# One planned PSUM placement and five reorderings of engine work in a two-block transformer kernel on one core

## The reference, cut to what matters

```
mod = c @ w_ada + b_ada                          # six rows: shift, scale, gate, twice
h = rms_norm(x, g) * (1 + sc1) + sh1
proj = h @ w_in                                  # q, k, v for compressed, selected, window and indexed attention
o_nsa = gates * (attention to compressed keys, to selected blocks, to a window)
score = sum_h w_idx[h] * relu(q_idx[h] @ k_idx.T)     # index scores, top 64 keys of a token kept
o_dsa = attention to the kept keys
x = x + gt1 * rms_norm(concat(o_nsa, o_dsa) @ w_out)
x = x + gt2 * rms_norm(square(relu(h2 @ w_up)) @ w_down)
# second block
proj = rms_norm(x) @ w_in_2                      # stick breaking attention, gated recurrence, memory attention
mixed = concat(rms_norm(sb_o), rms_norm(hg_o) * silu(g), mem_o)
x = x + mixed @ w_out_2
x = x + peer_ffn(rms_norm(x))                    # 8 heads pick 16 of 16384 experts each
```

## Time and profile before

| | us |
|---|---|
| median of 3 runs | 1515.25 |
| lowest, highest | 1513.32, 1517.54 |
| the profiled execution | 1512.21 |
| its span in the trace | 1510.4 |

### The profile page before, as it was taken

The page is one execution under the profiler, slowest core; times in us unless marked ns, Lnnn a source line. Parts: engine busy times, 40 slices in busy tenths (PEclk is TensorE's granted clock), DMA queues, the critical chain, the costliest instruction groups (busy, mean ns, idle before and its releaser), DMA issues.

```text
span 1510.4 us, 23097 instructions
## 1 busy us (share of the span) xinstructions
PE 1419.9 (94%) x9108; PEld 1230.4 (81%) x9108; DVE 873.0 (58%) x1501; ACT 745.1 (49%) x1368; POOL 981.9 (65%) x710
## 2 busy tenths in 40 slices
PE   5798998999998899899999999999999999999998
PEld 2676777799786897679998999899997888888886
DVE  5655773555524786621889939999894343322222
ACT  2442223666445657444554464455554555555554
POOL 0567624566764553145899998778886777766675
PEclk9896899999999999999999999999999999999999
DMA  9442223455654332034544555555656666555552
GB/s 382 150 167 112 112 112 140 167 172 190 253 197 165 140 118 106 28 112 170 206 171 156 175 186 184 179 181 179 203 182 218 234 248 244 208 185 182 192 195 84
DMA packets 48588, 263.78 MB, mean 175 GB/s; under 512 B 5472, under 2 KB 14048, under 8 KB 19040
## 3 DMA queue, kind: packets, MB, share of 16 engines
q1 hardware_dynamic: 38272, 251.68, 46.3%
q10 hardware_dynamic: 10208, 10.63, 2.0%
HBM read 252.84 MB, written 9.44 MB: 174 GB/s over the span
## 4 chain that ended last, share of the span: by engine, by line
PE 65%; DVE 16%; POOL 3%; issue 1%; ACT 1%; PEld 0%; PEldq 0%; DVEq 0%; ACTq 0%
PE bank L1381 24%; PE bank L788 22%; PE bank L752 16%; DVE arena L2613 4%; DVE hotg L2613 4%; DVE arena L2609 3%; POOL v_lo L1912 3%; DVE hots L2609 2%; PE bank L1161 1%; DVE arena L2625 1%; DVE arena L2495 1%; PE bank L769 0%; DVE hT_lo L1969 0%; PEld bank L788 0%; PE bank L1327 0%
## 5 line engine op out<-in xcount | busy, mean ns | idle before, releaser
L1912 POOL TENSOR_TENSOR v_lo<-ring,v_hi 128x512 fp32r<-128x512 f32 x448 | 620.3, 1402 | 168.9 <-ACT v_hi L1812 160.4
L1904 POOL TENSOR_TENSOR v_lo<-ring,d_hi 128x512 fp32r<-128x512 f32 x213 | 294.7, 1395 | 303.5 <-ACT d_hi L1503 238.1
L1812 ACT CAST v_hi<-ring 128x512 fp32r<-128x512 f32 x512 | 315.4, 621 | 307.7 <-PE bank L1381 164.3
L752 PE MATMUL bank<-hT_hi,v_hi 128*128 128x256 f32 x1024 | 294.8, 288 | 5.4 <-POOL v_lo L1912 5.3
L752 PE MATMUL bank<-hT_lo,v_hi 128*128 128x256 f32 x1024 | 286.3, 280 | 0.0
L752 PE MATMUL bank<-hT_hi,v_lo 128*128 128x256 f32 x1024 | 286.1, 279 | 0.0
L1503 ACT CAST d_hi<-ring 128x512 fp32r<-128x512 f32 x236 | 144.0, 621 | 172.3 <-PE bank L788 148.9
L1381 PE MATMUL bank<-v_hi,mix_hi 128*128 128x512 f32 x512 | 202.5, 396 | 3.2 <-DVE mix_lo L2640 3.2
L1381 PE MATMUL bank<-v_hi,mix_lo 128*128 128x512 f32 x512 | 201.9, 394 | 0.0
L1381 PE MATMUL bank<-v_lo,mix_hi 128*128 128x512 f32 x512 | 201.9, 394 | 0.0
L752 PEld LDWEIGHTS bank<-hT_hi,v_hi 128*128 128x128 f32 x1024 | 192.4, 188 | 7.1 <-POOL v_lo L1912 4.2
(11 more groups left out here) (329 smaller groups left out, 2437.5 us busy)
## 6 DMA issues: line engine op xcount, KB each, us to landing
ring<-w_dram SPq DMA_DIRECT2D x230, 1024.0 KB, 4.8
gate_dram<-gput ACTq DMA_DIRECT2D x64, 128.0 KB, 3.1
gget<-gate_dram SPq DMA_DIRECT2D x32, 256.0 KB, 5.0
x<-x_dram SPq DMA_DIRECT2D x1, 1024.0 KB, 5.5
arena<-mem_dram ACTq DMA_DIRECT2D x1, 1024.0 KB, 11.1
out_dram<-x SPq DMA_DIRECT2D x1, 1024.0 KB, 4.0
arena<-const_dram ACTq DMA_DIRECT2D x1, 884.0 KB, 9.3
arena<-vec_dram ACTq DMA_DIRECT2D x1, 144.0 KB, 4.5
```

The costliest lines, as they stand in the source:

```text
L752: return nc.tensor.matmul(out_, lhsT, rhs, start=start, stop=stop)
L1812: nc.scalar.copy(v_hi[:, r, :], quarter(at, r)).then_inc(s_vhi, 1)
L1904: nc.gpsimd.tensor_tensor(v_lo[:, r, :], dense_quarter(d, r), d_hi[:, r, :], ALU.subtract).then_inc(s_dpl, 1)
L1912: nc.gpsimd.tensor_tensor(v_lo[:, r, :], quarter(at, r), v_hi[:, r, :], ALU.subtract).then_inc(s_plo, 1)
```

## The change

Nothing is computed otherwise; instructions are placed elsewhere in their engines' lists, and one group of banks is fixed.

1. `h3T` gets the banks 5, 6, 7 and 2 (`H3_BANK`); the rotation counter goes on as before.
2. Head, ScalarE: the sines go between the two copies of the modulation rows, and the casts of ("in", 0, 0) go ahead of the wait for `s_gain`. Head, VectorE: the angles go ahead of the weighing of ("ada", 1, 1).
3. Compressed attention, VectorE: the scale factors `wsc` go ahead of the scores' wait; the row sums and masked probabilities go ahead of the index scores.
4. Behind attention, VectorE: `gain2` and `gg` go behind the two products and the first low parts; the coefficients of the last units are the reciprocals themselves, without a copy; one memset goes.
5. Second block, VectorE: the tables `iota16` and `iota4` are made ahead of `mixed_normed(0)` rather than behind the first head norm.
6. Second block, ScalarE: the casts of ("out2", 0, 1) go between `mixed_high(1)` and `mixed_high(2)`.

```diff
@@ -232,7 +232,9 @@
     for m in range(2, 4):
         rotate(("gg", m), [0, 1, 2, 3])
     rotate(("mkv", 1), every)
-    transposed("h3T")
+    for q in range(4):
+        group(("h3T", q), H3_BANK[q])
+    turn[0] += 4
     for t in range(13):
         for g, (name, bank) in enumerate(IN2_GROUPS.get(t, ())):
             group(name, bank)
@@ -304,6 +306,7 @@
 
 TAIL2 = [("memO",), ("ca", 0), ("ca", 1), ("sbo", 0), 0, ("ca", 2), ("hgx",), 1, ("ca", 3), 2, ("ca", 4), 3, ("hgo",),
          ("ca", 5), ("sbo", 1), 4, ("ssq", 0), ("ssq", 1), ("ca", 6), 5, ("ca", 7), 6, 7, ("ssq", 2)]
+H3_BANK = (5, 6, 7, 2)
 OUT2_BANK = {(0, 0): 2, (0, 1): 3, (1, 0): 5, (1, 1): 4}
 TAIL2_BANK = {("memO",): 2, ("hgx",): 4, ("hgo",): 5, ("sbo", 0): 1, ("sbo", 1): 6,
               ("ssq", 0): 7, ("ssq", 1): 4, ("ssq", 2): 7}
@@ -1534,19 +1537,18 @@
             ps = wait_full(act, ("adarow", 2))
             free(nc.scalar.copy(adarow[0:1, 0, :], ps[0:1, :]), ("adarow", 2))
             wait_read(act, ("adarow", 2))
-            ps = wait_full(act, ("adarow", 3))
-            free(nc.scalar.copy(adarow[0:1, 1, :], ps[0:1, :]), ("adarow", 3))
-            wait_read(act, ("adarow", 3))
-            nc.scalar.copy(stat[:, 152:153], one).then_inc(s_arc, 2)
-
             act.wait_ge(s_trig, 1)
             for src, dst, scale in ((trig[:, 3, :], sind[:, :, 32:64], 1.0), (trig[:, 3, :], sind[:, :, 0:32], -1.0),
                                     (trig[:, 5, :], cosd[:, :, 0:32], 1.0), (trig[:, 5, :], cosd[:, :, 32:64], 1.0)):
                 nc.scalar.activation(dst, src.rearrange("p (b f) -> p b f", b=TB), ACT.Sin,
                                      scale=scale).then_inc(s_sin, 1)
-
+            ps = wait_full(act, ("adarow", 3))
+            free(nc.scalar.copy(adarow[0:1, 1, :], ps[0:1, :]), ("adarow", 3))
+            wait_read(act, ("adarow", 3))
+            nc.scalar.copy(stat[:, 152:153], one).then_inc(s_arc, 2)
+
+            high_parts(("in", 0, 0))
             act.wait_ge(s_gain, 1)
-            high_parts(("in", 0, 0))
             features_high("h1T", gain1, mod[:, 0:KD])
             high_parts(("in", 2, 0))
             features_out("memT", vall("memg"))
@@ -1787,6 +1789,7 @@
             nc.scalar.activation(stat[:, 152:153], one, ACT.Sqrt)
             head_roots(2)
             mixed_high(1)
+            high_parts(("out2", 0, 1))
             mixed_high(2)
             high_parts(("out2", 1, 1))
             high_parts(("wq", 0, 0))
@@ -2062,8 +2065,6 @@
                 link(nc.vector.tensor_copy(kvT[w][:, 2, 0:32:2], vall(name)))
             link(nc.vector.tensor_copy(posf, posi))
             nc.vector.memset(coef[:, 0:1], 0.0).then_inc(s_const, 1)
-            weigh(("ada", 1, 1))
-
             def tr(i):
                 return trig[:, i, :]
             for tb in range(TB):
@@ -2079,7 +2080,7 @@
             link(ts(tr(3), tr(3), PI_IN, -PI_IN, ALU.min, ALU.max))
             ts(tr(5), tr(5), PI_IN, -PI_IN, ALU.min, ALU.max).then_inc(s_trig, 1)
 
-
+            weigh(("ada", 1, 1))
             ps = wait_full(dve, ("ada", 0))
             link(tt(mod[:, 0:16], ps[:, 0:16], vcol("b_ada", 0, 16), ALU.add))
             free(stt(gain1, mod[:, 8:16], 1.0, vall("g_pre_mix"), ALU.add, ALU.mult), ("ada", 0))
@@ -2133,6 +2134,8 @@
 
             def per_block(name):
                 return con(name).rearrange("p (b n) -> p b n", b=TB)[:, :, 0:N_CMP]
+            for tb in range(TB):
+                link(ts(wsc[:, tb, :], plain[:, tb, PL_WI:PL_WI + 4], IDX_SCALE, None, ALU.mult))
             for g in range(2):
                 ps = wait_full(dve, ("Sc", g))
                 for tb in range(TB):
@@ -2145,8 +2148,14 @@
             link(nc.vector.tensor_reduce(cmax, sv, AX.X, ALU.max))
             tt(sv, sv, cmax.unsqueeze(2).to_broadcast([P, 16, N_CMP]), ALU.subtract).then_inc(s_sc, 1)
 
+            dve.wait_ge(s_pc, 1)
+            link(nc.vector.tensor_reduce(lsum[:, 0:16], sv, AX.X, ALU.add))
             for tb in range(TB):
-                link(ts(wsc[:, tb, :], plain[:, tb, PL_WI:PL_WI + 4], IDX_SCALE, None, ALU.mult))
+                hs = slice(tb * HEADS, (tb + 1) * HEADS)
+                ins = tt(sv[:, hs, :], sv[:, hs, :],
+                         per_block("cmp01")[:, tb, :].unsqueeze(1).to_broadcast([P, HEADS, N_CMP]), ALU.mult)
+            ins.then_inc(s_pcz, 1)
+
             for tb in range(TB):
                 width = (tb + 1) * P
                 wait_read(dve, ("L", 2 * tb))
@@ -2159,14 +2168,6 @@
                         ins = stt(score[:, tb, 0:width], r, wsc[:, tb, h:h + 1], score[:, tb, 0:width],
                                   ALU.mult, ALU.add)
                     link(ins)
-
-            dve.wait_ge(s_pc, 1)
-            link(nc.vector.tensor_reduce(lsum[:, 0:16], sv, AX.X, ALU.add))
-            for tb in range(TB):
-                hs = slice(tb * HEADS, (tb + 1) * HEADS)
-                ins = tt(sv[:, hs, :], sv[:, hs, :],
-                         per_block("cmp01")[:, tb, :].unsqueeze(1).to_broadcast([P, HEADS, N_CMP]), ALU.mult)
-            ins.then_inc(s_pcz, 1)
             def key_round(i):
 
 
@@ -2263,15 +2264,14 @@
             attention(UNITS1, [(0, P), (P, P + T)], after1)
             for unit in UNITS1[-2:]:
                 wait_read(dve, ("PT", *unit))
-            link(stt(gain2, mod[:, 32:40], 1.0, vall("g_pre_ffn"), ALU.add, ALU.mult))
-            link(tt(gg[:, 0:8], mod[:, 16:24], vall("g_post_mix"), ALU.mult))
-            nc.vector.memset(coef[:, 0:1], 0.0).then_inc(s_ggf, 1)
-
-            coefficients("dsa", None)
+            a = KINDS["dsa"]
+            link(nc.vector.reciprocal(coef, lsum[:, a:a + 16]))
             for tb in range(TB):
                 weighted("dsa", ("O", "dsa", tb), tb, 512, False)
                 nc.vector.memset(stat[:, 153 + tb:154 + tb], 0.0).then_inc(s_o, 1)
             low_parts(("out", 0, 0))
+            link(stt(gain2, mod[:, 32:40], 1.0, vall("g_pre_ffn"), ALU.add, ALU.mult))
+            tt(gg[:, 0:8], mod[:, 16:24], vall("g_post_mix"), ALU.mult).then_inc(s_ggf, 1)
             features_low("oT", None)
             low_parts(("out", 1, 1))
             for n in range(2):
@@ -2327,8 +2327,6 @@
             wait_read(dve, ("mkv", 1))
             head_norm(mkv[:, 1, 0:T].rearrange("p (h d) -> p h d", h=4), 4, stat[:, 140:144], mqsq)
             nc.vector.memset(coef[:, 0:1], 0.0).then_inc(s_mksq, 1)
-            link(nc.vector.tensor_copy(iota16[:, :], iota[:, 0:TOPK]))
-            link(nc.vector.tensor_copy(iota4[:, :, :], iota[:, :].unsqueeze(2).to_broadcast([P, P, 4])))
             link(nc.vector.memset(hqe, 0.0))
             for part in hke:
                 link(nc.vector.memset(part, 0.0))
@@ -2511,6 +2509,8 @@
                               ALU.mult, ALU.subtract)
                 ins.then_inc(s_hlo, 1)
 
+            link(nc.vector.tensor_copy(iota16[:, :], iota[:, 0:TOPK]))
+            link(nc.vector.tensor_copy(iota4[:, :, :], iota[:, :].unsqueeze(2).to_broadcast([P, P, 4])))
             mixed_normed(0, ("hgo",))
             mixed_normed(1, ("sbo", 0))
             mixed_low(0)
```

## The result

| | before | changed |
|---|---|---|
| median of 4 runs each, us | 1514.28 | 1487.65 |
| lowest, highest | 1503.98, 1517.54 | 1485.29, 1497.99 |
| profiled execution, its span | 1512.21, 1510.4 | 1485.29, 1483.5 |

The account below looks back on a forecast made before the run. The kernel was taken as a string of matmul stages losing time at handovers, TensorE busy 94%. Terms 1.1 + 4.9 + 3.9 + 6.4 + 2.4 = 18.7 us, from 1515.25 to 1496.5 us; range 1488 to 1504.5.

Parts of the forecast that it names:

- head: Up to TensorE's first projection: starts 1.1 us earlier, 2.2 won less 1.1 for an operation caught by GpSimd.
- compressed attention: VectorE's order around the index scores: first unit's row maximum 4.9 us earlier, the transposes' 4.72 us wait gone.
- behind attention: After the last attention unit: transposes 3.2 us earlier, the projection 3.3 to 4.2 earlier, taken as 3.9 us.
- banks and tables: Second block's input: tile 0 starts 2.9 us earlier, the copies give 2.2; 6.4 us in all, bounds 4.6 and 7.5.
- high parts of the output: Second output tile: start 1.6 us earlier plus 0.8 of clock, 2.4 us, bounds 1.1 and 4.5.
- a microsecond won at a handover is simply kept: Whole kernel: work between handovers is TensorE back to back or starts when TensorE arrives, so gains last to the end.
- (a): Rival: half clock inside attention falls elsewhere, losing the 4.4 us dip (1492, chance 0.12) or adding one (1501, 0.09).
- (b): Rival: the VectorE-GpSimd port takes more, each passage gives its lower bound, 12.7 us, 1502.5; chance 0.08.
- (d): Rival: VectorE still orders the head and attention start, only the other passages win: 12.7 us, 1502; chance 0.04.
- (c): Rival: clock falls at the start of attention and stays down, up to 32 us more, 1528; chance 0.03.
- The sentence on the clock: Whole kernel: every gap shortened also gives clock back, toward 23 us in all, from the skill's throttled-by-default rule.
- the prediction's own sign of being wrong: Wrong if a named wait remains under another name, or half-clock stretches move the sum by over 5 us.

Follow-up runs that it names:

- the third run: Changed kernel with GpSimd's first wait put on the gain itself instead of on the modulation's sums; 1489.7 us.
- the fifth run: Changed kernel with VectorE's row sums and masked probabilities back behind the index scores; 1491.05 us, and when timed again median 1495.1, ratio 0.988.
- the seventh run: Changed kernel with the high parts of the second output tile behind mixed_high(2) again; 1499.6 us.
- ninth run: Changed kernel with GpSimd's first wait on the gain and filler matmuls behind the modulation and in attention's first two turns; median 1491.5 us, ratio 0.9824.

## Why the prediction was right, and where its sizes were off

The direction and the mechanism held; the size did not: 1487.65 is 8.9 us under the forecast of 1496.5 and 0.35 under the lower end of the range. By the means the change won 22.9 where 18.7 was forecast, a difference of 4 that lies within the interval of the measurement. Each edit undone by itself, beside its term of the sum:

| edit | forecast | handover | clock behind it | worth |
|---|---|---|---|---|
| head | 1.1 | 1.3 | 0 | 1.3 |
| compressed attention | 4.9 | 5.3 | 0 | 5.3 |
| behind attention | 3.9 | 3.3 | 3.7 | 7.0 |
| banks and tables | 6.4 | 5.0 | 3.5 | 8.5 |
| high parts of the output | 2.4 | 1.9 | 0 | 1.9 |
| sum | 18.7 | 16.8 | 7.2 | 24.0 |

Handover is the time at the waits and in VectorE's chain, clock the time lost in half-clock stretches that came back with the undone edit (1.0 + 0.6 + 2.2; 2.3 + 1.2). Each worth is one trace against the others. The sum of 24.0 stands against 22.9 and 21.6 measured in the two comparisons. It counts some time twice: on the step to tile 0 two edits undone by themselves cost 3.4 + 2.2 = 5.6, where both kernels' traces differ by 3.8 and 4.7, and on the step behind it 2.3 + 1.6 = 3.9, where they differ by 3.2. So the sizes in the table are good to a microsecond or two, and the clock's share more nearly 5 to 7 than a firm 7.2.

- **Head.** Right, 1.1 against 1.3, and for the reason given: the 128x8 operation is caught by GpSimd. The forecast's upper bound of 2.2 left that out, and the third run got 0.82 of it back. What no row could say, whether the weight tile is there when ScalarE wants it, went well: the casts started at 35.77.
- **Compressed attention.** Right, 5.1 to 5.3 against 4.9. The row maximum was worked out at 138.8, or 137.6 with the head's 1.2 taken off, and came at 137.49.
- **Behind attention.** The handover was right (3.26 + 0.97 against 3.2 + 0.7; the second term of both is full clock on the transposes). The step that failed is the sentence that a microsecond won at a handover is simply kept: here 2.8 us more were won behind it, the later dip standing some 45 us on, because the half clock behind the wait and the one on the up projection went with it.
- **Banks and tables.** Tile 0 won 3.4 for 2.9 (its wait alone 2.75), the copies 1.6 for 2.2. The forecast put 1.8 us of clock into this passage; undoing the two edits one by one gave 2.3 and a likely 1.2. The kernels themselves differ by less on that tile: 3.2 less the copies' 1.6 leaves 1.5 us of clock, near the 1.8. With all half clock gone, also behind the passage, the bound of 7.5 was the better value than 6.4.
- **Output.** The wait went from 3.69 to 1.88, 1.9 us for the 1.6 of the text; the 0.8 of clock that was counted on top is not shown, since the step behind it is 26.3 to 28.1 us with the edit and 27.7 to 28.9 without it.
- **Rivals.** (a), the dip inside attention lost, looked true in the first pair of traces (84.6 against 88.8, the 92.0 less the handover's 3.26). It was luck, in the sense of the next section. (b) and (d) fell by the rows: every wait went down as worked out, and the angles stand in VectorE's idle time. (c) did not come; the worst attention seen was 95.2, 10.6 above the best of the changed kernel, not 32.
- **The sentence on the clock.** "Every gap shortened here also gives clock back, toward 23 us in all" was written as an aside, and its 23 is what was measured (22.9); its direction is shown, that it agrees to a tenth is chance, with an interval of 10 us. (The upper bounds named add up to 23.3, not 23.4.) The sum held some 3.3 us of clock (0.7, 1.8 and 0.8); up to 7.2 came, some 4 more, and so the prediction's own sign of being wrong, clock moving the sum by over 5 us, was not reached. It failed as a term of the sum because the rows that could size it, the windows at 234 to 242, 278 to 282 and 504 to 511, were not set beside the waits in front of them.

## What stays luck

The step through the first attention, from the first unit's row maximum to the output's transposes, in traces whose instructions there are the same and stand in the same order:

| half clock in it, us | 0 | 3 | 10 | 17 | 17 | 17 | 20 | 20 | 27 | 27 |
|---|---|---|---|---|---|---|---|---|---|---|
| the step, us | 82.5 | 84.6 | 86.1 | 89.1 | 89.1 | 89.7 | 92.1 | 92.1 | 95.2 | 95.2 |

The two ends by window, first the fifth run (none), then the seventh (27 us):

```profile
160.00:170.00 10.00, 9.76 (x71) 7.70 (x71) 8.77 (x24) 2.62 (x12) 7.90 (x6) 1.00 0.16 47
```

```profile
160.00:170.00 10.00, 9.84 (x40) 7.84 (x41) 6.09 (x17) 0.91 (x4) 9.37 (x8) 0.50 0.00 0
```

TensorE is busy for over 97% of both windows, and gets through 71 matmuls in the one and 40 in the other (the seventh run is 5 us further on in its work there, so the two windows hold the same kind of turns, not the same ones). Over the whole step the difference is 12.7 us for one and the same piece of work, two thirds of the whole forecast, and likely much of why single runs of these kernels spread by 10 us or more. The dip came with the long wait ahead of it and without, and fillers in the first turns did not keep it away; its cause stays open.

## What to carry to other kernels

Before a wait is priced, look at the granted clock for the 50 us behind it, in two traces: a half-clock stretch that stands at the same place in both probably belongs to the wait and goes with it (here 5 to 7 us of time beside 17), one that moves or comes and goes belongs into the range. Undoing the edit by itself shows which it is. Small two-input VectorE operations on the path are cheap only while GpSimd is not subtracting: order them ahead of what releases GpSimd (0.17 us against 1.05 to 1.28 here). And a gain read from one pair of traces is worth little until each part has been undone by itself.

## What the hardware showed that was not expected

- A wait of 4.59 us ahead of 16 transposes brought half clock not only behind it (225 to 232) but again 40 us later, on the up projection (269 to 273); with the wait at 1.3 to 1.5 both were absent in all eleven traces.
- TensorE, busy for over 9.6 us of every 10 from 140 on (ninth run), fell to half clock at 156 for 20 us.
- The head differs between executions: in five of the fourteen traces, of either order, it had 13.6 us of half clock instead of 10 (3 in the ninth run, with fillers). In four of the five, all but the run with fillers ahead of the projection, the first projection came 1.6 to 3.1 us later than in the others of its order.
